# Conditioning projections of a decoder step: split fp32r pairs replaced by raw float32 in four TensorE column groups

## The reference

```python
sc = jax.nn.silu(c)
mods = (sc @ w_ada[l] + b_ada[l]).reshape(Bn, 3, 3, D)[:, :, :, None, :]
def mod(y, j):
    return rmsnorm(y, g_norm[l, j]) * (1 + mods[:, j, 1]) + mods[:, j, 0]
x = x + 0.5 * mods[:, 0, 2] * swiglu(mod(x, 0), w_ffn_gu[l, 0], w_ffn_down[l, 0])
```

## Time and profile before

| | |
|---|---|
| three runs | 2857.2, 2860.28, 2860.41 us; median 2860.28 |
| span of the profiled execution, first to last instruction | 2860.2 us |
| TensorE matmul busy | 2621.6 us, 92% |
| VectorE busy | 1296.3 us, 45% |
| ScalarE busy | 881.4 us, 31% |
| bytes moved | 294.25 MB, mean 103 GB/s |
| mean granted TensorE clock | 0.958 of full speed |

### The profile page before, as it was taken

How to read it: one execution, slowest core, us unless ns; L and a number is a source line. 1 busy time by engine, 2 the same in 40 slices (tenths; PEclk the granted TensorE clock), 3 DMA queues, 4 the chain that set the end, 5 groups by cost and what they waited for, 6 DMA issues and landing times.

```text
span 2860.2 us, 48702 instructions
## 1 busy us (share of the span) xinstructions
PE 2621.6 (92%) x20002; PEld 2407.8 (84%) x20002; DVE 1296.3 (45%) x1975; ACT 881.4 (31%) x1034; POOL 38.2 (1%) x64
## 2 busy tenths in 40 slices
PE   5799999899998689999987999996888999899997
PEld 4799999899998589999987999996763437899997
DVE  5544344556566854434446333345452223533333
ACT  4533133433334243313325212124333222321212
POOL 1000000000000000000000000000000000000000
PEclk9899999999999699999998999998999998999998
DMA  8344353333444125434432323221023332223321
GB/s 270 111 148 142 108 153 122 104 108 104 120 119 140 60 81 152 143 104 140 136 107 59 99 78 100 78 89 28 27 85 88 88 91 59 74 81 95 91 75 57
DMA packets 412517, 294.25 MB, mean 103 GB/s; under 512 B 35557, under 2 KB 408380, under 8 KB 412384
## 3 DMA queue, kind: packets, MB, share of 16 engines
q1 hardware_dynamic: 407456, 277.14, 32.6%
q0 software_dynamic: 4928, 15.30, 1.7%
HBM read 284.87 MB, written 7.51 MB: 102 GB/s over the span
## 4 chain that ended last, share of the span: by engine, by line
PE 84%; DVE 7%; ACT 3%; DMA 2%; issue 2%; SPq 1%; POOL 0%; DVEq 0%; ACTq 0%; POOLq 0%
PE ps L627 22%; PE ps L628 22%; PE ps L629 22%; PE ps L649 2%; PE ps L650 2%; PE ps L1173 2%; PE ps L870 2%; PE ps L1132 2%; PE ps L661 1%; PE ps L1133 1%; DMA raw<-in_hg_w_in 1%; DMA raw<-in_w_ada 1%; DVE rstd L1694 1%; DVE rstd L1899 1%; PE ps L1106 1%
## 5 line engine op out<-in xcount | busy, mean ns | idle before, releaser
L627 PE MATMUL ps<-hn_hi,w_hi 128*128 128x260 f32 x3680 | 1066.1, 290 | 49.4 <-DVE hn_lo L1710 47.1
L629 PE MATMUL ps<-hn_hi,w_lo 128*128 128x260 f32 x3680 | 1051.5, 286 | 0.0
L628 PE MATMUL ps<-hn_lo,w_hi 128*128 128x260 f32 x3680 | 1050.6, 285 | 0.0
L627 PEld LDWEIGHTS ps<-hn_hi,w_hi 128*128 128x128 f32 x3680 | 706.3, 192 | 55.4 <-issue 51.6
L1635 DVE TENSOR_TENSOR w_lo<-raw,w_hi 128x2048 fp32r<-128x2048 f32 (+5 forms) x280 | 564.3, 2016 | 316.7 <-ACT w_hi L1239 316.6
L629 PEld LDWEIGHTS ps<-hn_hi,w_lo 128*128 128x128 f32 x3680 | 706.0, 192 | 0.0
L628 PEld LDWEIGHTS ps<-hn_lo,w_hi 128*128 128x128 f32 x3680 | 705.8, 192 | 0.0
L1239 ACT ACTIVATE w_hi<-raw 128x2048 fp32r<-128x2048 f32 (+3 forms) x273 | 472.7, 1732 | 491.8 <-DMA raw<-in_w_ffn_gu 220.8
L628 PE MATMUL ps<-hid_lo,w_hi 128*128 128x260 f32 x1408 | 398.7, 283 | 0.0
L627 PE MATMUL ps<-hid_hi,w_hi 128*128 128x260 f32 x1408 | 397.9, 283 | 0.0
L629 PE MATMUL ps<-hid_hi,w_lo 128*128 128x260 f32 x1408 | 397.8, 283 | 0.0
(11 more groups left out here) (289 smaller groups left out, 2357.4 us busy)
## 6 DMA issues: line engine op xcount, KB each, us to landing
raw<-in_w_ffn_gu SPq DMA_DIRECT2D x176, 512.0 KB
raw<-in_w_ada SPq DMA_DIRECT2D x144, 512.0 KB
raw<-in_w_ffn_down SPq DMA_DIRECT2D x96, 384.0 KB
raw<-in_hg_w_in SPq DMA_DIRECT2D x32, 512.0 KB
pg<-in_cache_ckv SPq DMA_DIRECT2D x128, 128.0 KB, 2.0
raw<-in_w_ffn_down SPq DMA_DIRECT2D x32, 256.0 KB
raw<-in_kv_w_ada SPq DMA_DIRECT2D x16, 512.0 KB
ss<-in_state_hgrn POOLq DMA_DIRECT2D x8, 512.0 KB, 7.1
```

Source lines behind the costliest of these rows:

```text
L627: pe.matmul(out[:, t, :], wh, xh[:, c], start=start, stop=False)
L628: pe.matmul(out[:, t, :], wh, xl[:, c], start=False, stop=False)
L629: mm = pe.matmul(out[:, t, :], wl, xh[:, c], start=False, stop=stop)
```

## The change

A slab is now two row blocks (ADA_K = 2, so 256 input rows) of 1024 output columns, and four slabs make a round of eight column chunks of `mods`. There are 20 rounds, again 80 slabs of 1 MB. TensorE multiplies the raw float32 data: the stationary operand is `scz[:, k, :]`, nine columns of silu(c) padded with zeros to 32, and the 1024 output columns go as four pieces of 256 to the four 32-column groups of the array, each with its own 32 partitions of the PSUM bank (`tile_position`). For each slab, group 0 does both row blocks, then group 1, and so on: eight float32 matmuls. The slabs are not split; `rows` is [128, 256], copied once a round. A round is turned by two transposes, and VectorE adds the bias with two instructions. The slabs move: 8 lie ahead of the first FFN (before 14), 20 in each FFN of layer 0 (22), 4 in the first head's projections (2), 14 in the seven HGRN heads with projections (14), 2 in the last (6), 12 in the first FFN of layer 1 (none). The gates are made just ahead of the down projection or the output projection.

```diff
+ADA_K = 2
+ADA_S = KD // ADA_K
 ADA_W = 256
-ADA_L = 9 * D // ADA_W
+CG = 4
+GW = P // CG
...
-ADA_FIRST = 14
-ADA_FFN = MF
-ADA_TAIL = ADA_L - ADA_FFN - H
+ADA_FIRST = 2
+ADA_ROUNDS = {(0, 0): (3, 2), (0, 1): (3, 2), (1, 0): (3, 0), (1, 1): (0, 0)}
 def _stream():
-    def ffn(with_ada):
+    def ffn(l, j):
         out = []
-        for mn in (MFA, MFB):
-            out += [SLOT] * (mn * (2 if with_ada else 1)) + [mn // 2 * 256] * 8
+        for mn, rounds in zip((MFA, MFB), ADA_ROUNDS[l, j]):
+            out += [SLOT, 0] * (ADA_S * rounds) + [SLOT] * (mn - ADA_S * rounds) + [mn // 2 * 256] * 8
         return out
-    return ([SLOT] * ADA_FIRST + ffn(True) + [SLOT] * (4 * H + ADA_TAIL + 4) + ffn(True) + [SLOT, KD * P] + ffn(False)
-            + [SLOT, KD * P] + [QK * 384, RK * 256, RK * 256] * 4 + [RK * D] + [SLOT] * 4 + ffn(False))
+    hgrn = [SLOT, 0, 0, SLOT, 0, 0] + [SLOT, 0, SLOT, 0] * 7 + [0] * 2
+    return ([0] * (ADA_S * ADA_FIRST) + ffn(0, 0) + hgrn + [SLOT] * 4 + ffn(0, 1) + [SLOT, KD * P] + ffn(1, 0)
+            + [SLOT, KD * P] + [QK * 384, RK * 256, RK * 256] * 4 + [RK * D] + [SLOT] * 4 + ffn(1, 1))
...
-    return [("fresh", 0, 16), ("ada", 0, 0), ("tiles", 16, 8), ("comb", 0, 0), ("tiles", 24, 8), ("ada", 1, 0),
-            ("comb", 1, 0)]
+    return [("fresh", 0, 16), ("ada", 0, 0), ("ada", 1, 0), ("tiles", 16, 16), ("ada", 2, 0), ("ada", 3, 0),
+            ("comb", 0, 0)]
...
-        sc18 = place("sc18", [P, KD, 2 * SEQS], F32R)
+        scz = place("scz", [P, KD, GW])
...
+            def ada(view, col, s):
+                columns(view, col, D, ADA_K * s, ADA_K)
+            def ffn(l, j, view=None, col=0):
+                for m0, mn, kn, rounds in ((0, MFA, MFA // 2, ADA_ROUNDS[l, j][0]),
+                                           (MFA, MFB, MFB // 2, ADA_ROUNDS[l, j][1])):
+                    if rounds:
+                        with T.loop(sp, rounds, {"slot": 2 * ADA_S}) as i:
+                            for q in range(ADA_S):
+                                gate_up(gu_v[l, j], i * ADA_S + (m0 + q))
+                                ada(view, i * D + col, q)
+                        col += rounds * D
...
+            for j in range(ADA_FIRST):
+                for s in range(ADA_S):
+                    ada(ada_v[0], j * D, s)
+            ffn(0, 0, ada_v[0], ADA_FIRST * D)
+            for g in range(2):
+                hgrn_project(0, 2 * g)
+                ada(ada_v[0], 7 * D, 2 * g)
+                ada(ada_v[0], 7 * D, 2 * g + 1)
+            for n, (view, col) in enumerate(((ada_v[0], 8 * D), (kvada_v, 0), (kvada_v, D))):
                 for q in range(2):
-                    hgrn_project(i * 2 + (q + 1))
-            hgrn_project(7)
-            for j in range(ADA_TAIL):
-                columns(ada_v[1], (H + j) * ADA_W, ADA_W)
+                    for g in range(2):
+                        hgrn_project(2 * n + q + 1, 2 * g)
+                        ada(view, col, 2 * q + g)
+            for g in range(2):
+                hgrn_project(7, 2 * g)
+                ada(ada_v[1], 0, g)
+            for s in range(2, ADA_S):
+                ada(ada_v[1], 0, s)
...
-            def ada():
-                hi, lo = slabs(KD, ADA_W)
-                if T.n.get("ada", 0) or T.i is not None:
+            def ada(slab):
+                k0 = T.n.get("slot", 0)
+                turns = LAND * (k0 // RAW + 1)
+                if T.i is not None:
+                    turns = T.i * (LAND * T.per["slot"] // RAW) + turns
+                pe.wait_ge(landed[k0 % RAW], turns)
+                if slab == 0 and (T.n.get("ada", 0) or T.i is not None):
                     pe.wait_ge(rows_copied, T.at("ada"))
-                split()
-                for k in range(KD):
-                    pe.matmul(ps[0:18, 6, 0:ADA_W], sc18[:, k, :], hi[:, k, :], start=(k == 0), stop=False)
-                    mm = pe.matmul(ps[0:18, 6, 0:ADA_W], sc18[:, k, :], lo[:, k, :], start=False, stop=(k == 7))
+                w = raw[k0 % RAW][:].rearrange("p (k n) -> p k n", k=ADA_K)
+                for g in range(CG):
+                    for kk in range(ADA_K):
+                        k = ADA_K * slab + kk
+                        mm = pe.matmul(ps[g * GW:(g + 1) * GW, 6, 0:ADA_W], scz[:, k, :],
+                                       w[:, kk, g * ADA_W:(g + 1) * ADA_W], start=(k == 0), stop=(k == KD - 1),
+                                       tile_position=(0, g * GW))
                 mm.then_inc(slot_used, 1)
                 T.add("slot")
-                T.add("ada")
+                if slab == ADA_S - 1:
+                    T.add("ada")
...
-                    mm = pe.matmul(ps[:, 7, j * SEQS:(j + 1) * SEQS], rows[:, j * P:(j + 1) * P], comb,
-                                   start=True, stop=True)
+                    mm = pe.transpose(ps[:, 7, j * P:(j + 1) * P], rows[:, j * P:(j + 1) * P], ident)
...
+            def ffn(l, j):
+                due = False
                 for half, mn in ((0, MFA), (1, MFB)):
-                    by_hand = 2 if with_ada else mn % 4 or 4
+                    rounds = ADA_ROUNDS[l, j][half]
+                    if rounds:
+                        for m in range(ADA_S):
+                            hidden(half == 0 and m == 0, due and m == 0, m == 0)
+                            ada(m)
+                        due = True
+                        with T.loop(pe, rounds - 1, {"slot": 2 * ADA_S, "lo": ADA_S, "up": ADA_S, "ada": 1, "comb": 1}):
+                            for m in range(ADA_S):
+                                hidden(False, m == 0)
+                                ada(m)
...
+                if n:
+                    r = k % RAW
+                    turns = LAND * (k // RAW + 1)
+                    if T.i is not None:
+                        turns = T.i * (LAND * T.per["split"] // RAW) + turns
+                    act.wait_ge(landed[r], turns)
+                    act.activation(w_hi[:, r, 0:n], raw[r][:, 0:n], ACT.Copy).then_inc(hi_done, 1)
                 T.add("split")
-            def ada():
+            def ada(slab):
                 split_hi()
-                act.wait_ge(slot_used, T.at("slot", 1))
-                if T.n.get("ada", 0):
-                    act.wait_ge(comb_done, T.at("ada"))
-                act.activation(rows[:], ps[0:2 * SEQS, 6, 0:ADA_W], ACT.Copy).then_inc(rows_copied, 1)
+                if slab == ADA_S - 1:
+                    act.wait_ge(slot_used, T.at("slot", 1))
+                    if T.n.get("ada", 0) or T.i is not None:
+                        act.wait_ge(comb_done, T.at("ada"))
+                    act.activation(rows[:], ps[:, 6, 0:ADA_W], ACT.Copy).then_inc(rows_copied, 1)
+                    T.add("ada")
...
+                for b in range(2):
+                    cols = mods[:, bass.ds(col, 8), :].rearrange("p (g b) s -> p g b s", b=2)
+                    added = bias[:, bass.ds(col, 8)].rearrange("p (g b) -> p g b", b=2)
+                    ins = dve.tensor_tensor(cols[:, :, b, :],
+                                            ps[:, 7, b * P:(b + 1) * P].rearrange("p (g s) -> p g s", g=CG)[:, :, 0:SEQS],
+                                            added[:, :, b].unsqueeze(2).broadcast_to([P, CG, SEQS]), ALU.add)
+                ins.then_inc(mods_added, 1)
...
+            def make_gate(base, factor):
+                dve.wait_ge(mods_added, T.at("comb"))
+                if T.n.get("res", 0):
+                    dve.wait_ge(x_upd, T.at("res", 2, 2))
+                link(dve.tensor_scalar(gate[:], mods[:, base:base + KD, :].rearrange("p c s -> p (c s)"), factor, None,
+                                       ALU.mult))
...
+            def ffn(l, j, gate_base, col=0):
+                due = None
                 for half, mn in ((0, MFA), (1, MFB)):
-                    if col is None:
-                        for m in range(mn):
-                            hidden(m)
-                    else:
-                        for m in range(2):
-                            with_ada(m)
-                            done += 1
-                        with T.loop(dve, (mn - 4) // 2, {"slot": 4, "split": 4, "up": 2, "comb": 2, "chain": 2}) as i:
-                            for q in range(2):
-                                hidden(i * 2 + (2 + q), i * 4 + (col + 2 * (done - 1 + q)))
-                                split_lo()
-                                T.add("slot")
-                        done += mn - 4
-                        for m in range(mn - 2, mn):
-                            with_ada(m)
-                            done += 1
+                    rounds = ADA_ROUNDS[l, j][half]
+                    for n in range(rounds):
+                        for m in range(ADA_S):
+                            hidden(n * ADA_S + m, due)
+                            ada_slot()
+                            due = None
+                        due, col = col, col + 8
```

(43 more changed lines are left out.)

262 lines of the change are left out of this document (92 added, 170 removed).

## The result

| | before | after |
|---|---|---|
| median, us | 2860.35 (2857.2 to 2860.8, 4 runs) | 2773.39 (2768.66 to 2777.13, 4 runs) |
| profiled span, us | 2860.2 | 2767.1 |
| mean granted clock | 0.958 | 0.952 |

The ratio is 0.9698 (interval 0.9685 to 0.9712): 87 us faster, where 30 slower was forecast. It lies in the range, 8 us from the time of rival A.

The account below looks back on a forecast made before the run. TensorE was taken to bound most of the kernel (84% of the chain), loads the first slabs. Start, FFNs, first head's projections, heads and last head: -27 + 15 + 38 + 8 + 5 - 9 = +30, giving 2890 us; range 2755 to 2945.

Parts of the forecast that it names:

- rival A: Slabs: each column group has its own queue, so groups overlap; 1.17 us a slab, 2765 us in all; chance 0.26.
- matmuls start in the order of the program: Slabs: a group starts only after the previous group's last pass has started; 13 passes, 2.82 us a slab.
- 71 bare slabs: Slabs whose full TensorE time was counted: 63 in FFNs and heads, 71 with the start.
- nearer to the serial row than to the ideal: Slab's 2.82 us set against bounds: 3.47 with all passes in line, 0.87 with four groups always side by side.
- The pass of 0.216: Slab matmuls: each float32 matmul is two passes of 0.216 us, a slab sixteen.
- The switches at 0.3: Around a slab: changing the array between 128 and 32 columns costs 0.3 us, the middle of 0 to 0.6.
- Start: Before the first FFN: eight slabs at TensorE's own pace, squares added at 55 instead of 82.87; -27 us.
- Layer-0 FFNs: Two FFNs with 20 slabs each: +7.3 us each, +15 together.
- layer 1's first FFN: The FFN that had no slabs gets 12 at TensorE's full price: +38 us.
- Heads: Seven HGRN heads: first slab lies beside an unchanged chain, second is bare at +0.7 us each; +5 in all.
- Last head: Four of six VectorE splits leave its chain, 2.17 us each: -9 us.
- Nothing for bias, gates, splits in the FFNs and DMAs: Later gates, two bias additions, dropped FFN splits and the slabs' loads: no change in time.

Follow-up runs that it names:

- widths: Changed kernel with group g streaming 256 - 32g columns, the left-out columns not computed; 2767.83 us (1 run).
- fence: Changed kernel with one more TensorE wait, already met, between a slab's column groups, so the build can't reorder across it; 2772.33 us, ratio 0.9699.
- twice: Changed kernel with each group doing its two row blocks twice in a row, eight passes a group; 2985.69 us (1 run).
- four_times: Changed kernel with each group doing its two row blocks four times in a row, sixteen passes a group; 3540.79 us (1 run).
- twice_mixed: Changed kernel with the same doubled work as twice, but the column groups in the inner loop; 2812.01 us (1 run).
- k_outer: Changed kernel with a slab's two loops swapped, row block outside and column group inside; 2767.85 us, ratio 0.9679.
- one_group: Changed kernel with all eight matmuls of a slab in column group 0 and one result; 2921.4 us (1 run).
- late_split: Changed kernel with the next head's weights split at tile 24 instead of 16 in the HGRN heads; 2738.97 us, ratio 0.9564.

## Why the prediction was wrong

**The step that failed** is "matmuls start in the order of the program. If that holds across groups, group 1 can start only when group 0's last pass has started: each of three changes of group hides one pass, 16 - 3 = 13 passes, 2.82 us". It doesn't hold across groups (*widths*, and *fence* for the order of the program). A group holds four passes, the running one among them (*twice*, *four_times*, *twice_mixed*), and this change gives each group four before it turns to the next. So all four groups run at once, and the slab is 4 steps, 0.87 us, not 13 and 2.82. Over the prediction's 71 bare slabs that is 71 x 1.95 = 138 us, of which the start, bound by loads and a weight tile, keeps some 11. The forecast missed the profiled span by 123 and the median by 117.

Two things were weak in it. The rows that I called evidence all had matmuls on the whole array, where a queue for each group can't show; they spoke for neither side. And I took it as a reason that 2.82 "lies nearer to the serial row than to the ideal", when these two were only bounds, and the break-even, 2.7 us a slab, lay just under my figure (14% under 3.1, not the 15% that stands there). A was given 0.26 and named what decides; the evidence would have borne about as much for it as for mine.

In the traces passes of four groups begin 13 ns apart (7 in *k_outer*) and run together. The Trainium skill, "TensorE: Matmul & The Clock Gate", part 3 (What overlaps and what doesn't), has the overlap right. Its rule that starts and ends keep program order is contradicted across column groups by *widths*, and the measurement decides. The Trainium skill, "TensorEngine Tiling (Array Packing)", Key Properties, has a drain at each change of mode. The 0.33 us a slab agrees with that, at about half of my upper bound; that a drain is what it is made of, no run shows.

**The other steps.**
- The pass of 0.216 and two passes a matmul: right (*one_group*).
- The switches at 0.3: measured 0.33 to 0.35.
- Start: 31.9 saved for 27 (83 - 55 is 28, a slip of 1). The mechanism was wrong: what ended it was not TensorE at its own pace but a weight tile's landing and its splits.
- Layer-0 FFNs, layer 1's first FFN: within 0.6 us each with A's slab.
- Heads: the fixed chain held, 11.4 us. That the first slab lies beside it was right; that the second is bare was not (*one_group*). With shorter slabs the heads got 22.5 us of waits, for 15.3, and a low clock behind each.
- Last head: the four splits left the chain.
- Nothing for bias, gates, splits in the FFNs and DMAs: the FFNs come out without a term for them, and what lies outside the stages differs by 1 to 2 us.

**Open.** Whether the four places are counted in passes or in matmuls of two passes can't be told here: every step of the program put an even number into a group.

## What to carry to other kernels

Small float32 products that use 32 of 128 columns are cheap in four column groups, whatever their order, as long as no group gets more than four passes (two float32 matmuls) in a row; beyond that put the groups in the inner loop. These are float32 matmuls with 160 to 256 moving columns; other types and widths were not run. A row about matmuls on the whole array says nothing on how column groups queue, so treat such a rule as open. After a change, look for what an engine's in-order program puts ahead of urgent work: splits that waited for a landing, at the start and in the heads, were worth 49 us once the slabs were fast. A wait that TensorE no longer has can be worth more than its length, when the clock is low behind it.

## What the runs showed that was not expected

- A column group holds four passes, one of them running; the fifth stops all that stands behind it, the other groups' passes too (20 steps a slab in *twice*, 52 in *four_times*, and 8 in *twice_mixed*, where the other groups already have theirs when one gets its fifth).
- Each group goes at the pace of its own width beside the others: the group of 160 columns has its third pass running when that of 256 has its second (*widths*).
- Weight loads for 32 columns stay hidden even in one group: each pass has its own, and the passes still follow each other in 0.216 us (*one_group*).
- Taking 3.75 us of wait from each head gave 6: the rest is the granted clock, 1.00 in the heads for 0.93 to 0.96 (*late_split*).
